# A slot of gathered expert rows: one expert of 128 tokens, or four experts of each of 32 tokens

## The reference

```
s = einsum('mhpc,hpnc->mhpn', q, sub_keys)          # 8 heads, 2 halves, 128 keys
top_s, top_i = top_k(s, 16)
cand_s = top_s[:, :, 0, :, None] + top_s[:, :, 1, None, :]
best_s, best_c = top_k(cand_s, 16)                  # 16 of 256 pairs; ids follow
g = softmax(best_s)
act = gelu(einsum('nkd,nd->nk', u[ids], x)) * g     # x: the normed token
out = einsum('nk,nkd->nd', act, v[ids])             # added to the residual
```

## Time and profile before

| | us |
|---|---|
| median of three runs | 3054.7 |
| the profiled execution | 3051.98 |
| its span | 3050.2 |

### The profile page before, as it was taken

One profiled execution on the slowest core, in us unless ns is written; L12 is line 12 of the kernel. 1 busy time (PEld: TensorE's weight loads), 2 busy tenths in 40 slices (PEclk: granted clock), 3 DMA queues, 4 the chain that ended last, 5 costly groups with the idle time before them and its releaser, 6 DMA issues.

```text
span 3050.2 us, 34985 instructions
## 1 busy us (share of the span) xinstructions
PE 2672.8 (88%) x11992; PEld 2179.5 (71%) x11992; DVE 2159.5 (71%) x6642; ACT 638.2 (21%) x1693; POOL 994.4 (33%) x1028
## 2 busy tenths in 40 slices
PE   8889999999977888989997898889997887777787
PEld 6778888788855776868876676768885556555555
DVE  1237777787877678777778668767779668779565
ACT  3221313712111205202111204301221101102001
POOL 0002323333233333333234333333234333433332
PEclk9899999999999999999999999999999999999999
DMA  5249999999999999999999999999999999999997
GB/s 183 98 148 405 381 383 397 390 406 407 390 403 427 405 425 393 402 426 407 390 409 423 427 427 405 392 427 407 405 380 423 427 426 422 424 416 417 427 424 332
DMA packets 166642, 1182.34 MB, mean 388 GB/s; under 512 B 19376, under 2 KB 19904, under 8 KB 23872
## 3 DMA queue, kind: packets, MB, share of 16 engines
q0 software_dynamic: 147456, 1073.81, 85.6%
q1 hardware_dynamic: 19008, 106.31, 9.0%
HBM read 1177.95 MB, written 2.10 MB: 387 GB/s over the span
## 4 chain that ended last, share of the span: by engine, by line
PE 59%; DMA 22%; DVE 11%; issue 7%; ACT 2%; POOL 0%; DVEq 0%; SPq 0%; ACTq 0%; POOLq 0%
PE main_bank L318 36%; DMA main_ring<-in_uv,main_idi 22%; PE main_bank L354 12%; PE main_bank L352 6%; DVE main_diagonal L301 3%; DVE main_ring L287 2%; PE main_bank L522 1%; DVE main_pick L193 1%; DVE main_hid L287 1%; PE main_bank L714 1%; DVE main_pick L199 1%; PE main_bank L730 1%; PE main_bank L722 0%; DVE main_topi L162 0%; DVE main_work L154 0%
## 5 line engine op out<-in xcount | busy, mean ns | idle before, releaser
L318 PE MATMUL main_bank<-main_ring,main_diagonal 128*128 128x256 f32 (+1 forms) x8160 | 1981.1, 389 | 337.5 <-DVE main_diagonal L301 335.0
L318 PEld LDWEIGHTS main_bank<-main_ring,main_diagonal 128*128 128x128 f32 x8160 | 1526.1, 192 | 713.5 <-DVE main_diagonal L301 495.7
L287 DVE CUSTOM_DVE_ANT_0 main_ring<-main_ring,main_bank 128x1024 f32<-128x1024 f32 x1024 | 1248.5, 1219 | 634.4 <-DMA main_ring<-in_uv,main_idi 624.2
L270 POOL DMA_INDIRECT main_ring<-in_uv,main_idi x1024 | 994.2, 971 | 2031.9 <-PE main_bank L318 1781.1
L292 ACT ACTIVATE main_act_out<-main_hid 128x1 f32<-128x1 f32 x1024 | 206.8, 203 | 2140.6 <-DVE main_hid L287 2133.1
L301 DVE TENSOR_SCALAR main_diagonal<-main_ident,main_act_out,main_gate 128x128 f32<-128x128 f32 x1024 | 359.6, 351 | 43.7 <-PE main_bank L318 23.8
L354 PE MATMUL main_bank<-main_xT,main_w_block 128*128 128x256 f32 x1408 | 350.2, 381 | 1.8 <-ACT main_xT L387 1.8
L354 PEld LDWEIGHTS main_bank<-main_xT,main_w_block 128*128 128x128 f32 x1408 | 267.6, 191 | 38.4 <-ACT main_xT L387 2.2
L354 PE MATMUL main_bank<-main_xT_query,main_w_block 128*128 128x256 f32 x512 | 122.9, 379 | 0.9 <-ACT main_xT_query L387 0.9
L354 PEld LDWEIGHTS main_bank<-main_xT_query,main_w_block 128*128 128x128 f32 x512 | 96.5, 190 | 13.9 <-ACT main_xT_query L387 1.2
L292 ACT ACT_TABLE_LOAD x81 | 103.9, 1283 | 1.4
(11 more groups left out here) (187 smaller groups left out, 1212.9 us busy)
## 6 DMA issues: line engine op xcount, KB each, us to landing
main_w_block<-in_w_query SPq DMA_DIRECT2D x32, 1024.0 KB
main_w_block<-in_w_ab SPq DMA_DIRECT2D x24, 1024.0 KB
main_ring<-in_uv,main_idi POOLq DMA_INDIRECT x1024
main_w_block<-in_w_c_in SPq DMA_DIRECT2D x16, 1024.0 KB
main_w_block<-in_w_out SPq DMA_DIRECT2D x8, 1024.0 KB
main_w_block<-in_w_c_out SPq DMA_DIRECT2D x8, 1024.0 KB
main_att_bias<-in_att_bias SPq DMA_DIRECT2D x16, 256.0 KB, 6.0
main_resid<-in_x SPq DMA_DIRECT2D x2, 1024.0 KB, 7.5
```

The source lines that it names most:

```text
L270: nc.gpsimd.indirect_dma_start(self.ring[n % self.bufs], None, self.uv[p // NT], bass.IndirectOffsetOnAxis(self.choice.idi[:, p % 2, k:k + ...
L287: self.nc.vector.tensor_tensor_reduce(out=row, in0=row, in1=self.ps[:, 6:8], scale=1.0, scalar=0.0, op0=ALU.mult, op1=ALU.add, accum_out=s ...
L318: last = self.nc.tensor.matmul(self.ps[:, 4 + at // T, at % T:at % T + wide], self.diagonal[:, n % DIAGS], self.ring[n % self.bufs][:, D + ...
```

## The change

A slot now holds four experts of each of 32 tokens. Partition 32e + i holds expert e of the four for token 32j + i; j counts the groups of 32 tokens in a block. A group has 32 slots (`SHARE`), so there are 32 groups G in all. The ids and the gates are written in this order by 16 copies of 32x8 each for every pair of heads. Each of the four groups of a block needs ids of all four pairs, 8 slots (`EACH`) of each.

The weight matrix of a slot, `lhs`, has 32 columns in place of 128: a repeated identity times GeLU times gate; there are as many as ring buffers, not three. Each of the four products of a slot covers 256 of the 1024 columns of v and writes to another quarter of PSUM's partitions, all in bank 4. The `add` takes the four quarters to the residual, four instructions a group.

The normed row of a token must stand in all four quarters. PE makes the copies: a product of a 32x128 matrix `spread` (the repeated identity times the tokens' scale, made by ACT) with the 32 tokens' residual, two halves of 512 columns for each group. DVE multiplies each half by the gain in place. Three banks serve: the first half of the next group is made in the middle of the current group (PE at slot 16, DVE at slot 22), the other half at its end. That one needs a bank which the current group's dot products still read, so PE waits for the last of them.

The order changes too. Two pairs and four heads are done before the first slot (before: one pair and three heads). The choice for the next block is now always complete within the current one (`pair_at`, `head_at`). The second half of layer 0's mixer starts at slot 17 in place of 24 (`IN_AT`), and its transposes and gains move from before the loop to slots 12 to 15.

```diff
-        slots, heads = slice(2 * g * PK, (2 * g + 2) * PK), slice(2 * g, 2 * g + 2)
-        nc.vector.tensor_copy(self.idi[:, p % 2, slots], self.idf[:]).then_inc(self.chosen, 1)
+        heads = slice(2 * g, 2 * g + 2)
+        for e in range(QUADS):
+            for j in range(QUADS):
+                last = nc.vector.tensor_copy(self.idi[TB * e:TB * e + TB, p % 2, self.slots(g, j)], self.idf[TB * j:TB * j + TB, self.EACH * e:self.EACH * e + self.EACH])
+        last.then_inc(self.chosen, 1)
...
-        nc.vector.tensor_tensor(self.gate[:, p % 2, 2 * g * PK:(2 * g + 2) * PK].rearrange("p (h k) -> p h k", h=2), self.best[:, heads],
-                                self.den[:, heads].unsqueeze(2).to_broadcast([P, 2, PK]), ALU.mult).then_inc(self.gated, 1)
+        for e in range(QUADS):
+            h, at = 2 * g + e * self.EACH // PK, e * self.EACH % PK
+            for j in range(QUADS):
+                tokens = slice(TB * j, TB * j + TB)
+                last = nc.vector.tensor_scalar(self.gate[TB * e:TB * e + TB, p % 2, self.slots(g, j)], self.best[tokens, h, at:at + self.EACH],
+                                               self.den[tokens, h:h + 1], None, ALU.mult)
+        last.then_inc(self.gated, 1)
...
+    def copy_rows(self, pe, G, late):
+        p, j = divmod(G, QUADS)
+        (a, b), tokens = self.half(G, late), slice(TB * j, TB * j + TB)
+        pe.wait_ge(self.spreads, G + 1)
+        if G >= (1 if late else 2):
+            pe.wait_ge(self.dotted, SHARE * (G if late else G - 1))
+        self.nc.tensor.matmul(self.ps[:, b], self.spread[tokens], self.resid[tokens, p % NT, a * T:(a + 1) * T], start=True, stop=True).then_inc(self.copied, 1)
+
+    def gain_rows(self, dve, G, late):
...
+        dve.wait_ge(self.copied, 2 * G + late + 1)
+        self.nc.vector.tensor_tensor(self.ps[:, b], self.ps[:, b], self.gain[p // NT][:, a * T:(a + 1) * T], ALU.mult).then_inc(self.x_there, 1)
...
-        self.nc.vector.tensor_scalar(self.diagonal[:, n % DIAGS], self.ident[:], self.act_out[:, k:k + 1],
+        self.nc.vector.tensor_scalar(self.lhs[:, n % self.bufs], self.rep[:, 0:TB], self.act_out[:, r:r + 1],
                                      self.choice.gate[:, p % 2, k:k + 1], ALU.mult, ALU.mult).then_inc(self.placed, 1)
...
+        for a in range(QUADS):
+            rows = self.resid[tokens, p % NT, a * BC:(a + 1) * BC]
+            last = self.nc.vector.tensor_tensor(rows, self.ps[TB * a:TB * a + TB, 4, 0:BC], rows, ALU.add)
+        last.then_inc(self.added, 1)
...
-        wide = T if k == 0 else BC
-        for a in range(D // wide):
-            at = a * wide
-            last = self.nc.tensor.matmul(self.ps[:, 4 + at // T, at % T:at % T + wide], self.diagonal[:, n % DIAGS],
-                                         self.ring[n % self.bufs][:, D + at:D + at + wide], start=k == 0, stop=k == HK - 1 and at % T + wide == T)
+        for a in range(QUADS):
+            last = self.nc.tensor.matmul(self.ps[TB * a:TB * a + TB, 4, 0:BC], self.lhs[:, n % self.bufs],
+                                         self.ring[n % self.bufs][:, D + a * BC:D + (a + 1) * BC], start=r == 0, stop=r == SHARE - 1)
...
-PAIR_AT = ((47, 60, 78, 98), (52, 72, 130, 150))
-HEAD_AT = ((45, 51, 58, 64, 76, 82, 96, 102), (52, 55, 72, 75, 130, 133, 150, 153))
-ATT_AT = 88
+LATER = (47, 60, 78, 98), (16, 58, 72, 106)
+HEADS = (45, 51, 58, 64, 76, 82, 96, 102)
+SECOND = (24, 52, 90, 106)
+IN_AT = 17
+ATT_AT = IN_AT + 64
...
                 for k in range(HK):
+                    G, r = divmod(p * HK + k, SHARE)
+                    if G and r == 0:
+                        experts.place(dve, (G - 1) // QUADS, (k - 1) % HK)
+                        experts.gain_rows(dve, G, True)
                     experts.dot(dve, p, k)
...
+                    if r == SHARE - 1 and G + 1 < 2 * NT * QUADS:
+                        experts.copy_rows(pe, G + 1, True)
                     experts.sum_rows(pe, p, k)
+                    if r == 16 and G + 1 < 2 * NT * QUADS:
+                        experts.copy_rows(pe, G + 1, False)
```

More of the change, by code:

```diff
@@ L115, with slots @@
     PAIRS = PH // 2
+    EACH = 2 * PK // QUADS
+    def slots(self, g, j):
+        return slice(SHARE * j + self.EACH * g, SHARE * j + self.EACH * (g + 1))
     def __init__(self, nc, s, consts, scores, room):
@@ L272, in pool, with spread_scale @@
                                                  self.landed[n % self.bufs], 16)
-    def row_inputs(self, dve, p):
-        c = p % NT
-        dve.wait_ge(self.gain_in, 16 if p < NT else 48)
[L277 to L281, removed]
+    def spread_scale(self, act, G):
+        p, j = divmod(G, QUADS)
+        n, tokens = p // 2 * 2 + 1, slice(TB * j, TB * j + TB)
+        act.wait_ge(self.norms.scaled, n + 1)
+        if p:
+            act.wait_ge(self.copied, 2 * (G - QUADS) + 2)
+        self.nc.scalar.activation(self.spread[tokens], self.rep[tokens], ACT.Copy, scale=self.norms.rs[tokens, n, p % 2:p % 2 + 1]).then_inc(self.spreads, 1)
@@ L1236, in trunk @@
         gain_rows = [gain0[:], place("gain1", 11296, [P, D])[:], place("gain2", 14848, [P, D])[:]]
-        scale = lambda p: norms.rs[:, p // 2 * 2 + 1, p % 2:p % 2 + 1]
-        experts = Experts(nc, s, choice, A, consts, bank, resid, scale, gain_rows, [ring[:, k] for k in range(BUFS)], room)
+        experts = Experts(nc, s, choice, A, consts, bank, resid, norms, gain_rows, [ring[:, k] for k in range(BUFS)], room)
         mix1 = Recurrent(nc, s, A, weights, norms, tail1, bank, xT, xb, own("gate_x", 0, [P, RT, HALF]), xc, own("i_gate", 2048, [P, RT, HALF]),
@@ L1321, in _ @@
             norms.root_mean(act, 1)
-            act.wait_ge(loaded[1], 32)
+            act.wait_ge(loaded[1], 48)
             for t in range(2):
@@ L1326, in _ @@
             norms.rows_scaled(act, 2, mix0.rows[1])
-            for i in range(4):
+            experts.spread_scale(act, 0)
+            for i in range(5):
                 tail0.act_q(act, 0, i)
@@ L1547, in _ @@
             experts.place(dve, 2 * NT - 1, HK - 1)
-            experts.add(dve, 2 * NT - 1)
+            experts.add(dve, 2 * NT * QUADS - 1)
             final.mean_dve(dve, NT - 1)
@@ L1579, in _ @@
             tail0.pe_turn(pe, 0, 3)
-            for i in range(4):
+            for i in range(6):
                 tail0.pe_query(pe, 0, i)
-            pe.wait_ge(tail0.s_taken, 3)
-            pe.wait_ge(weights.taken, tail0.firsts[0] + 8)
-            mix0.turn_pe(pe, 1)
+                if i == 1:
+                    experts.copy_rows(pe, 0, False)
+                    experts.copy_rows(pe, 0, True)
             for p in range(2 * NT):
@@ L1592, in _ @@
-                        for x in paced(k, 2, 4 * weights.PIECES):
-                            tail0.pe_query_piece(pe, 0, 4 * weights.PIECES + x)
-                        if k == 26:
-                            tail0.pe_scores(pe, 0, PH - 1)
-                        for x in paced(k, 24, mix0.IN * weights.PIECES):
+                        if k < 8:
+                            for x in range(4 * k, 4 * k + 4):
+                                tail0.pe_query_piece(pe, 0, 6 * weights.PIECES + x)
@@ L1613, in _ @@
+                        u, odd = divmod(k - ATT_AT, 2)
+                        if not odd and 0 <= u < 2 * AH + 2:
                             mix0.att_pe(pe, 1, u)
```

251 lines of the change are left out of this document (139 added, 112 removed).

## The result

The changed kernel takes 3170.3 us (median; 3163.0 to 3176.8), the kernel before 3054.8 on the same chip: 1.038 times as long (95% interval 1.0355 to 1.0403). It is slower by 115 us; I had forecast 21 faster and said at most 3085. The profiled execution took 3172.5 for a span of 3170.6, so the spans differ by 120.

The account below looks back on a forecast made before the run. DMA was taken as the bound (floor 2698 us for eight blocks), PE in places. Block terms and tail summed to -21 us, span 3050.2 to 3029, so 3034 forecast against 3054.7; own range 3015 to 3053, whole range 2968 to 3085.

Parts of the forecast that it names:

- Rival (b): Group edges make DVE the bound, each costing 2.5 us instead of 1 in seven blocks: about 3068 us; chance 0.22.
- DVE's need per block: DVE's forecast busy time in each block, 207 to 340 us, under the floor each time, 94% of it in p = 0.
- the floor of DMA: The eight blocks' unchanged bytes at 427 GB/s: 2698 us for 2817, so at most some 119 us come back.
- The ring: Seven gather slots, 17.2 us, leave 5.3 us spare (6.5 with a shorter sum), hiding an edge alone, not beside a pair's step.
- The sign that I had named for (b): In p = 2 and 4, DMA's rate falling below 400 GB/s would show DVE to be the bound.
- Small instructions: 16 casts and 16 gate products a pair on DVE, 0.18 us each: +5.4 us a pair, +21.6 a block.
- Dots: DVE's pitch between dots in a burst falls from 1.40 to 1.28 us with the smaller matrix: -15 us a block.
- The edge: At each group's end DVE waits 2 to 4 us for PE's late copy; 1 us charged in loaded blocks, none in p = 7.
- rival (c): PE's four column quarters don't run at once, a paced slot takes 3.3 us for 3.0: about 3115 us; chance 0.06.
- The start and the end: First dot at 247 us for 224.6, p = 0 +11 us, p = 7 316 us, the tail -1.
- Rival (a): DMA runs at its floor everywhere, with DVE's extra work hidden: about 2978 us; chance 0.20.
- The point of 90%: DVE decides the time once its busy share over a group passes some 90%; p = 0, 2 and 4 stood there.

Follow-up runs that it names:

- e5: Changed kernel with one cast and one gate product a pair and no late row copy or its gain product after the first group: 3018.0 us, ratio 0.9871.
- e10: Changed kernel with only the pairs' slots in p = 2, 4 and 6 moved (4, 24, 60, 106 for 16, 58, 72, 106): 3146.5 us, ratio 1.0292.
- e2: Changed kernel with one cast and one gate product of 128x32 a pair in place of 16 and 16: 3044.0 us, ratio 0.9955.
- e3: Changed kernel without the late half of the row copies and its gain product from the second group on: 3108.1 us, ratio 1.0166.
- e11: Changed kernel with all four products of a slot written to the first quarter, one after another: 3405.2 us, ratio 1.1138.
- e12: e5 with products of zeros added to keep PE busy, three a slot without dense pieces, one with them: 3030.1 us, ratio 0.9911.
- e4: Kernel before with each pair's cast and gate product split into 16 instructions of 32x8 each: 3107.4 us, ratio 1.0159.
- e1: Changed kernel with products of zeros after each slot's sum but a group's last, three without dense pieces, one with them: 3241.5 us, ratio 1.061.

## Why the prediction was wrong

Rival (b) named the mechanism and the side, with 0.22; its price was 13 us where 115 came. Point by point:

*The step that failed* is the comparison of DVE's need per block with the floor of DMA ("under the floor each time"), by which the small instructions and most of an edge were taken as hidden, and the one microsecond charged for an edge. Measured, the two cost 152 us together (e5): 126 and 62 alone. The need itself was near: 340, 268, 302, 267, 299, 268, 271, 207 us forecast, 354, 282, 310, 281, 306, 281, 279, 197 measured. (The terms for p = 0 add up to 343. The 207 for p = 7 counts small instructions, though no pair stands there; without them it is 185.) But p = 6 had 271 us of forecast work against a floor of 317, and I gave it 320; it took 337. The ring covers some 5 us by my own estimate, not a block: reserve in a block's calm groups is of no use to its loaded ones; e10 shows this (24 us from placing alone). The third groups of p = 2, 4 and 6, where it failed most, grew by 17.5, 18.6 and 11.2 us; a sum by groups of 32 slots was the one to make. That it is DVE's work, e2 and e5 show. Block by block the miss is +38 in p = 0, +15 to +17 in p = 1 to 4 and 6, +25 in p = 5, none in p = 7. Without the small instructions and the late copy (e5) the blocks took 378.5, 356, 347, 350, 347, 345, 322 and 319 us, where I had forecast 382, 359, 351, 349, 349, 343, 320 and 316: the sum was that of a kernel in which these two are hidden. The sign that I had named for (b) came: DMA's rate in p = 2 and 4 is 393 and 394 GB/s, under 400, and POOL's wait for the sum grew (1881.0 us for 1781.1) instead of shrinking. Blocks 1, 3 and 5 grew by 4, 5 and 12 us instead of shrinking by 10 to 13.

*Small instructions.* Forecast +5.4 us a pair. Measured, as the mean of all 32 pairs from the first start to the last end, 2.9 us for 16 casts and 4.0 for 16 gate products; one of each took 0.18 and 0.19 before, so +6.5. In the lines above a cast is 0.175 from start to start (2.62 for 15) and a gate product 0.26 (3.95 for 15). The gate product has a scalar from memory, and the row I took (L209) was a cast's. The error of 1.1 us a pair, some 36 in all, is less than what the whole cost where it was on the path: 126 us for 32 pairs, 3.9 each. The Trainium skill, "VectorE: DVE Perf Modes", section "Two Vector instructions with no wait between them", has an instruction held until all earlier ones have finished when its start quadrant differs from the last one's. The trace agrees, as the casts start 0.175 us apart, as long as one alone lasts (0.18), and not 0.095 as in the earlier trace rows.

*Dots.* The pitch is 1.35 to 1.36 us, not 1.28: the placing takes 0.303 on average where it took 0.351. I had scaled by elements from a long addition, to a pitch of 1.30 that I rounded down to 1.28; in fact a quarter of the columns still took 86% of the time. Forecast -15 us a block, measured about -6.

*The group.* Two gain products 1.4 and the additions 1.71: 3.1, forecast 3.0. Right.

*The edge.* Mean wait 3.4 us (104.0 over 31), forecast 2 to 4. Right in size, wrong in what it displaces: 62 us for 31 edges (e3), of which only 26 remain when DVE has room (e5 against e2). The copy took 1.12 us at the high clock and 2.07 at the low one, not 0.86, so that the waits in p = 6 and 7, without dense pieces, were 2.9 us each. (The terms that I gave add up to T + 2.5 and T + 3.8, not 2.7 and 4.)

*PE.* The quarters run at once (e11), so rival (c) is refuted. The sum takes 0.64 us at the high clock, as forecast 0.6, and 1.08 at the low one. I had said nothing of the clock: the earlier trace rows show 0.98 to 1.00 throughout, and how the clock goes when PE idles between sums was not in them. The Trainium skill, "TensorE: Matmul & The Clock Gate", section "Part 1: The HAM clock gate", says that throttled is the resting state and that activity releases it. The trace agrees with that (0.50 in p = 6 and 7, where PE has only the sums; 0.96 there with e12's zero products). By e12 the low clock costs next to nothing where DVE has room; through the edges it may have some 20 us of the 115 (the estimate under e12), which no run shows by itself.

*The start and the end.* First dot at 245.8, forecast 247; p = 7 315.5, forecast 316; the tail -1.2, forecast -1. In p = 0 the first 32 slots, with the two pairs and POOL's waits for their ids, took 112.4 us for the 97 that I had, the other groups 103.1, 101.2 and 103.1 for 93.5, 93 and 98.

*Rival (a)* needed the extra work to be hidden. Even e5 lies 40 us above its 2978.

*The point of 90%* in rival (b) is near, but the share alone doesn't order the groups: the third of p = 1 took as long as before at 86%, that of p = 2 17.5 us more at 90%, that of p = 6 11.2 more at 93%.

## What to carry to other kernels

Compare an engine's need with the bound over the length that the buffers cover, not over a stage: p = 6, with DVE at 83%, lost 19 us, 11 of them in its one group at 93%. Work that moves off a relieved engine onto the one with the next highest share must be priced as if it were on the path unless a window of the ring's length shows the room; here some 190 us cost 50 in the kernel with more room and 126 in the one with less. Rearranging across partitions is paid per instruction rather than per element (a cast of 32x8 takes 0.17 us, one of 128x32 0.18): give it to an idle engine, and move the bunches apart, before counting on what the rearrangement buys.

## What the hardware showed unexpectedly

- Casts of 32x8 cost 0.17 us each on DVE and 0.21 on ACT, products of 32x8 with a scalar from memory 0.24 and 0.30. Moving from one quarter to another costs nothing on top (173 and 237 ns in e4, 170 and 236 in the changed kernel; in both, each instruction reads another quarter than the one in front of it).
- Four products side by side in 32-column quarters took 0.64 us for 8 passes of 256 columns at the high clock, one after another 1.91.
- PE freed from work ran at half its clock (0.50) for 650 us, and its sums took 1.08 us instead of 0.64, the copies 2.07 instead of 1.12. Filling it with products of zeros brought the clock back and made the kernel 71 us slower (e1), 12 us in the lighter version (e12).
